# Down-projection weights of a mixture of experts issued from a second DMA queue, behind the gathers

## What is computed

```
def moe_ffn(h, w_rg, b_rg, w_re, b_re, w_g, w_u, w_d):
    ...                                  # top-1 group of 4, top-2 experts of its 8
    slot_tok = jnp.full((P,), N, jnp.int32).at[dest].set(tok_sorted)
    h_pad = jnp.concatenate([h, jnp.zeros((1, D), h.dtype)], axis=0)
    xb = h_pad[slot_tok].reshape(n_blk, EXPERT_BLOCK, D)     # a gather of rows
    ...
    def run(args):
        xe, e = args
        return (jax.nn.silu(xe @ w_g[e]) * (xe @ w_u[e])) @ w_d[e]
    ...
    y_assign = yb[dest].astype(jnp.float32) * flat_w[order][:, None]
    return jax.ops.segment_sum(y_assign, tok_sorted, num_segments=N).astype(h.dtype)
```

## Time and profile before

| | us |
|---|---|
| median of 3 runs | 953.1 |
| lowest and highest | 952.74, 953.22 |
| the profiled execution, its own time | 962.63 |
| span of its trace | 960.8 |
| stretch of the 32 experts on TensorE, first gate matmul to last down matmul | 420.55 to 885.50 |

### The profile page before, as it was taken

How to read it: one execution, slowest core, us unless ns; L and a number is a source line. 1 busy time by engine, 2 the same in 40 slices (tenths; PEclk the granted TensorE clock), 3 DMA queues, 4 the chain that set the end, 5 groups by cost and what they waited for, 6 DMA issues and landing times.

```text
span 960.8 us, 11382 instructions
## 1 busy us (share of the span) xinstructions
PE 932.7 (97%) x4433; PEld 471.1 (49%) x4433; DVE 547.1 (57%) x1125; ACT 195.2 (20%) x428; POOL 61.8 (6%) x70
## 2 busy tenths in 40 slices
PE   9999999999999999999999999999999999999998
PEld 6565767877554444644343344334333333333443
DVE  3116330637876411564777787777777676767434
ACT  3111210003656301421111111111111111111401
POOL 3100060000000000010000000000000000000000
PEclk9999998999999999999999999999999999999999
DMA  8690452340002793678999999999999999999311
GB/s 300 216 297 1 129 153 78 107 152 2 1 1 72 211 415 118 248 267 347 419 418 419 419 419 421 418 419 419 419 419 420 419 419 420 419 422 386 128 44 50
DMA packets 74874, 260.57 MB, mean 271 GB/s; under 512 B 12554, under 2 KB 36502, under 8 KB 49956
## 3 DMA queue, kind: packets, MB, share of 16 engines
q1 hardware_dynamic: 69568, 248.51, 66.4%
q0 software_dynamic: 4080, 8.93, 2.7%
q10 hardware_dynamic: 1172, 2.40, 0.6%
HBM read 252.72 MB, written 13.08 MB: 277 GB/s over the span
## 4 chain that ended last, share of the span: by engine, by line
PE 76%; SPq 16%; DMA 4%; DVE 2%; issue 1%; ACT 0%; POOLq 0%; DVEq 0%
PE ps L1123 69%; SPq L377 16%; DMA w<-in_w_exp_down 3%; PE ps L1504 2%; PE ps L1774 1%; PE ps L1147 1%; PE ps L1809 0%; PE ps L1158 0%; DMA xg<-hn_rows,sidx 0%; DMA gmix<-in_norm_mix 0%; PE ps L1507 0%; PE ps L1244 0%; PE ps L1313 0%; DVE probs L2336 0%; PE ps L1329 0%
## 5 line engine op out<-in xcount | busy, mean ns | idle before, releaser
L1123 PE MATMUL ps<-w,xe 128*64 128x512 f32 x1024 | 229.4, 596 | 11.8 <-DMA w<-in_w_exp_up 10.5
L2710 DVE TENSOR_TENSOR h<-h,ps 128x1024 f32<-128x1024 f32 x120 | 143.2, 1215 | 112.8 <-PE ps L1123 112.7
L1123 PEld LDWEIGHTS ps<-w,xe 128*64 128x64 f32 x1024 | 69.6, 137 | 152.8 <-issue 130.3
L1123 PE MATMUL ps<-w,hT 128*64 128x512 f32 x504 | 115.4, 599 | 1.4 <-DMA w<-in_w_exp_down 1.4
L1123 PE MATMUL ps<-yk,ST 128*128 128x512 f32 (+1 forms) x320 | 105.3, 431 | 0.7 <-DVE yk L2700 0.5
L1123 PE MATMUL ps<-xT,wring 128*128 128x272 f32 x384 | 102.0, 406 | 0.0
L1123 PEld LDWEIGHTS ps<-xT,wring 128*128 128x128 f32 x384 | 69.8, 193 | 25.7 <-issue 12.6
L1123 PE MATMUL ps<-wring,xT 128*32 128x128 f32 (+2 forms) x368 | 77.7, 404 | 0.4 <-DVE xT L2005 0.4
L1123 PEld LDWEIGHTS ps<-yk,ST 128*128 128x128 f32 (+1 forms) x320 | 48.6, 174 | 56.9 <-issue 26.7
L1072 ACT ACTIVATE sg<-ps 64x256 f32<-64x256 f32 x64 | 24.1, 377 | 257.8 <-PE ps L1123 245.7
L755 POOL DMA_INDIRECT xg<-hn_rows,sidx x32 | 31.9, 998 | 655.6 <-PE ps L1774 371.8
(11 more groups left out here) (364 smaller groups left out, 871.9 us busy)
## 6 DMA issues: line engine op xcount, KB each, us to landing
w<-in_w_exp_gate SPq DMA_DIRECT2D x64, 1024.0 KB, 24.9
w<-in_w_exp_up SPq DMA_DIRECT2D x64, 1024.0 KB, 26.8
w<-in_w_exp_down SPq DMA_DIRECT2D x63, 1024.0 KB, 25.8
wring<-in_w_in SPq DMA_DIRECT2D x12, 512.0 KB, 6.6
wpg<-in_w_ple_gate SPq DMA_DIRECT2D x2, 2048.0 KB, 12.2
biaslines<-blrow SPq DMA_DIRECT2D x1, 2560.0 KB, 10.8
h<-in_x_prompt SPq DMA_DIRECT2D x4, 512.0 KB, 7.9
wring<-in_w_in SPq DMA_DIRECT2D x2, 1024.0 KB, 7.1
```

Of the source, the lines that this page charges most:

```text
L1123: return nc.tensor.matmul(out, l, r, start=start, stop=stop, skip_group_check=skip)
L2710: TTn(h[0:r, t, :], h[0:r, t, :], both(b, r), ALU.add).then_inc(S["hadd"], 1)
```

## The change

The down pieces of all experts move from SyncE's queue to GpSimd's. For experts 0 to 2 they are issued before the gathers, behind the same semaphores as before. From expert 3 on, `load_d(J)` stands behind `gather(J)`: GpSimd waits for `d_done` to show expert J-3's down matmuls done, issues D0 and D1 of expert J, and then waits for `x_tr` to issue `gather(J+1)`. An overflow job's down pieces move in the same way. Gate and up pieces stay with SyncE's queue, now back to back. No piece changes in size, place or semaphore, and nothing changes on TensorE, VectorE or ScalarE.

```
@@ -594,7 +594,7 @@
             sp.wait_ge(S["ot_ok"], TP)
-            for i in (G0, G1, U0, U1, D0, D1):
+            for i in (G0, G1, U0, U1):
                 load_piece(sp, 0, i, 0)
@@ -613,11 +613,8 @@
             sp.wait_ge(S["op_done"], summed(TP - 1))
-            load_piece(sp, 1, D0, 1)
             load_piece(sp, 2, U1, 2)
-            load_piece(sp, 2, D0, 2)
             sp.wait_ge(S["sq_done"], 2 * TT)
-            load_piece(sp, 1, D1, 1)
@@ -631,11 +628,6 @@
-            def load_d(J):
-                sp.wait_ge(S["d_done"], J - 2)
-                load_piece(sp, J % 3, D0, J)
-                load_piece(sp, J % 3, D1, J)
@@ -657,8 +649,6 @@
             for J in range(4, NE):
                 load_gu(J)
-                load_d(J - 1)
-            load_d(NE - 1)
@@ -743,6 +733,21 @@
             pool.wait_ge(S["kc_in"], 16 * NB)
             pool.wait_ge(S["vc_in"], 16 * NB)
+
+            pool.wait_ge(S["ot_ok"], TP)
+            load_piece(pool, 0, D0, 0)
+            load_piece(pool, 0, D1, 0)
+            pool.wait_ge(S["op_done"], summed(TP - 1))
+            load_piece(pool, 1, D0, 1)
+            load_piece(pool, 2, D0, 2)
+            pool.wait_ge(S["sq_done"], 2 * TT)
+            load_piece(pool, 1, D1, 1)
+
+            def load_d(J):
+                pool.wait_ge(S["d_done"], J - 2)
+                load_piece(pool, J % 3, D0, J)
+                load_piece(pool, J % 3, D1, J)
+
             pool.wait_ge(S["hn_out"], 16 * TT)
@@ -760,6 +765,8 @@
                 if J >= 2:
                     pool.wait_ge(S["x_tr"], J - 1)
                 gather(J, sidx[:, J:J + 1])
+                if J >= 3:
+                    load_d(J)
```

More of the change, by code:

```diff
@@ L681, in load_job @@
                 sp.wait_ge(S["d_done"], J)
-                for i in (G0, U0, G1, U1, D0, D1):
+                for i in (G0, U0, G1, U1):
                     load_piece(sp, OVSLOT, i, e)
@@ L773, in gather_job @@
                 gather(J, icur[:, 0:1])
+                e = pool.value_load(jtab[0:1, bass.ds(J, 1)], min_val=0, max_val=NE - 1)
+                pool.wait_ge(S["d_done"], J)
+                load_piece(pool, OVSLOT, D0, e)
+                load_piece(pool, OVSLOT, D1, e)
             overflow(pool, nov, gather_job)
```

## The result

The changed kernel takes **963.15 us** (median of 4 runs, 962.76 to 965.28), the kernel before beside it 953.16 us (4 runs, 952.74 to 953.73). The ratio is 1.0104, 95% interval 1.0092 to 1.0116: it is 10.0 us slower. The profiled execution took 962.97 us.

A forecast was written before the change was run, and what follows sets the result against it. The prediction took the DMA engines' weight stream as the bound, with TensorE nearly even. Terms of +8.5 at the loop's end and +1.3 for the mixed stream, +9.8 on 953.1, gave 962.9 us, range 954 to 977.

The forecast's parts named there:

- Same bytes, same end of the stream, 0: Experts' loop: the saturated stretch starts at the same time, carries the same bytes and ends at about 881.3 us; cost 0.
- So the end is its landing plus 3.65 plus 9.09: Loop's end: after the last landing at 881.3, TensorE's remaining work ends down(31) at 894.0 instead of 885.5, +8.5 us.
- a mixed stream: Loop's weight stream: 58 down pieces beside SyncE's queue each cost 0.02 us more, +1.3 us.
- They push the gate and up pieces back by one down pair, waits begin four experts earlier, at 16: Loop's middle: early down pieces delay gate and up by 5.1 us, so TensorE's waits start at about expert 16.
- Half of the engines, a pair in 17 us: Loop's down pieces: with half of the engines an expert's pair lands in 17 us instead of 25.
- Gathers, 0: GpSimd's queue: gathers wait behind the down pair but land with 5 us slack, if the pair takes at most 15; 0.
- Profile and median: Whole kernel: the median lies 9.5 us under the profiled execution's 962.63, and that difference was carried over to the forecast.
- finishing together: Rival, loop's end: down pieces get a third of the engines, +3 to +4 us, 956 to 958; chance 0.12.
- nothing: Rival, whole loop: engines serve in issue order or earlier waits are taken back, 953.1 us; chance 0.07.
- faster: Rival, weight stream: two queues give more than one, 949 to 951 us at 432 GB/s; chance 0.10.
- a slower stream: Rival, whole weight stream: each per cent slower costs 4.4 us, 967 for 1%, 977 for 3%; chance 0.19.
- a late gather: Rival, loop's gathers: a pair over 15 us makes TensorE wait, 980 to 990 us at 1 us over; chance 0.04.

The follow-up runs named there:

- early_only: Changed kernel with the loop's down pieces back on SyncE's queue, only those of experts 0 to 2 staying on GpSimd's: 954.07 us, ratio 1.0006.
- before_again: Kernel before, unchanged, run for a second trace: 959.73 us in one execution.
- Last2_sync: Changed kernel with the down pieces of experts 30 and 31 back on SyncE, last in its queue: 968.29 us, ratio 1.0079.
- hold_one: Changed kernel with GpSimd issuing every down pair from expert 3 on one expert later: 960.47 us, ratio 1.0068.
- f1: Kernel before, one queue, from expert 4 on down pieces issued between their own expert's two gate/up pairs: 977.04 us, ratio 1.0184.
- loop_only: Changed kernel with the first three experts' down pieces back on SyncE's queue, the loop's staying on GpSimd's: 964.17 us, ratio 1.0101.
- first and third group: Follow-up runs sharing a chip per group; the kernel before took 962.0 us on the first group's chip, 959.5 on the third's.

## Why the prediction was right, and where it was not

**The time and the sign**: 962.9 predicted, 963.15 measured. The largest term is of the right size and from the right cause (down pieces pass gate and up), but it was put at the wrong place.

- *Same bytes, same end of the stream, 0*: right within 1 to 2 us. The rate in the loop is 416 to 420. The gap that I took to stay does stay: 223 GB/s in 426.38 to 431.38, the same place behind the loop's start, against 229. The changed loop had 0.39 MB more than early_only by +80 (0.21 counted from the same lead), worth 0.5 to 0.9 us. Last landing: 871.7 - 412.93 = +458.8, against 881.2 - 420.55 = +460.7.
- *The last to land is expert 31's `b` pair*: true. *So the end is its landing plus 3.65 plus 9.09*: **the step that failed**. TensorE came to it 1.8 us after it had landed. It was late from expert 30's `b` pair, which had been passed by four down pieces (9.7 us against early_only), and 28.2 us of its own work lie behind that. The step rests on the lag of one pair. With 5.1 us, b(30) would give 434.9 + 5.1 + 28.2 = +468.2, and the last landing, at 894.0 - 420.55 = +473.5, would have been the later bound. With the lag of two pairs b(30) gives 434.9 + 10.2 + 28.2 = +473.3; measured is +473.1. So two things were missed: that two pairs pass, and that the end has to be asked of each of the last experts and not of the last piece alone.
- Why both give +8 to +9: from b(30) to b(31) only some 1.5 down pieces are left to pass (5.45 MB in all, 1.53 of them GpSimd's queue's), so these pairs land 13.9 us apart (+444.9 to +458.8), against 15.7 of TensorE's between their starts, and the two bounds lie 1.8 us apart. It was luck that they are so near. Against the old trace the loop grew by 8.2 us where I said 8.5: b(30) is 10.0 later and 1.8 are won back, 1.36 of them the wait for D(30) that has gone. Against early_only it grew by 8.9 and against before_again by 9.5; the medians differ by 10.0. The forecast's 9.8 has the 1.3 us of a mixed stream in it, which were not there, so that the total fits within 0.3 us is luck too.
- *They push the gate and up pieces back by one down pair, waits begin four experts earlier, at 16*: the first wait is at expert 15. But the lag is not one pair, and the four experts came out nearly right because two errors offset each other. At b(15) the lag is 8.8 us, not 5.1. And the lead is used up faster than I took it to be: in early_only b(15) lands at +203.7, 8.2 us before TensorE would come to it, and five experts later TensorE waits, so it loses 1.6 us per expert there, not 1.26. The waits are also uneven: 2.27 and 4.43 us at experts 16 and 19, nothing between.
- *Half of the engines, a pair in 17 us*: no row of before shows the half, and the 17 us are worked out from it. In the changed kernel it is half: in 830 to 834 us, with a down pair on its way, GpSimd's queue has 49.3% of the engines and SyncE's 51.0%. 17 is too long; 11.9 is the median. I had charged both the 4 us until the queue is served and the full share. Order of issue over both queues would by my estimate have given 25 us and more, from the 25.3 to 27.9 us that down pieces took before, and an unchanged time.
- *Gathers, 0*: right, 15.0 us median to landing, 16.3 at most, and no wait at the transposes beyond the first gather's. *SyncE and GpSimd can hold the issues*: right, 548 ns a piece, not the 1 us of a gather.
- *A mixed stream costs 1.3 us*: not seen. Queues 1 and 0 together move what one did, 419 GB/s in 480 to 840 us in both traces.
- *Profile and median*: I carried 9.5 us of difference over. It is not the profiler: 7.6 of it are the stall ahead of the loop, which nine of the 14 traces have and five have not (last section). The changed kernel's profiled run lies 0.2 us from its median.
- *Its signs*: the last wait is not the one before expert 31's second half, and down pieces land in 11.9 us, not in 15 to 19. One sign of being wrong, down(31) ending by 887, is met by the letter: it ends at 886.07. That is so because this trace's loop starts 7.6 us earlier; on the clock of the old one it would be 893.7, and near 894 was said.
- *Rivals*: finishing together (a third of the engines) is out by the 11.9 us; nothing and faster by the interval; a slower stream by the rate (419 GB/s before and after); a late gather by the waits.

Last2_sync and hold_one were my own theory's test and it fell there: expected near the time of before, measured 1.0079 and 1.0068.

## What to carry to other kernels

When a stream of weights is the bound, a second queue added no bandwidth here (416 to 420 GB/s with one or two); its pieces passed those of the first (11.9 us to landing, against 31.0 and 36.6 for gate and up), and the stage that needed its weights first was late by it all along (7.8 to 10.9 us at each `b` pair from 12 to 30): keep pieces in one queue in the order of use. Compute the end as the latest, over the last stages, of a stage's landing plus all work behind it, not from the last landing alone. And before a load is moved up in a queue, look at what it waits for, since what stands behind it waits too: in f1 that left 228 GB/s for 20 us, where it was 399.

## What I had not expected of the hardware

- In the changed kernel the same 16 matmuls took longer behind its three waits of over 2 us: 5.32 us behind 2.27, 6.64 behind 4.43, 5.33 behind 2.29, instead of 3.65. The page shows a clock slice under full there, and the stretch 672.9 to 692.9 a granted clock of 0.92. Not always: in f1 a wait of 2.75 us was followed by 3.65, and in loop_only five of 2.27 to 2.36 were, while one of 2.43 was followed by 5.33. No run isolates this, and the sums above don't need it: the stream, not TensorE, sets the next landing.
- SyncE's queue was less deep in f1, and the stream was no faster for it: there down pieces land after 13.3 us and up pieces after 20.2, in the changed kernel 11.9 and 36.6, at the same 419 GB/s.
- The stall ahead of the loop is not explained. It is in the profiled execution of before and in all eight traces of the first and third group, whichever queue has the down pieces: TensorE is busy for 12.95 to 14.80 of the 17 us from 141 to 158, in the other five traces for all of them. With it the loops start at 416.02 to 420.73, without it at 412.45 to 414.47. The runs of before on these two groups' chips are also the longer ones (medians 962.0 and 959.5, against 954.2). So it goes with the chip or its state, as far as these traces show, and not with the change. It has no part in the result: loops are compared from their own start.
